# Branch hints for the expert jumps of a mixture-of-experts stage, on three engines

## What is computed

```
logits = xt @ w_router + b_router            # 256 tokens, 32 experts
top_val, top_idx = top_k(logits, 4)          # each token goes to 4 experts
gates = softmax(top_val)
for each expert e, for its tokens xb:
    hdn  = xb @ w_up[e] + b_up[e]            # 1024 -> 2048
    gate = minimum(hdn[:, :1024], 7); up = clip(hdn[:, 1024:], -7, 7)
    act  = (up + 1) * gate * sigmoid(1.702 * gate)
    y    = act @ w_down[e] + b_down[e]       # 1024 -> 1024
    out[token] += gate_of_token * y
```

## Time and profile before

| | us |
|---|---|
| median of 3 runs | 2451.59 |
| lowest and highest | 2449.55, 2455.35 |
| the profiled execution | 2454.41 |
| its span, first to last instruction | 2452.5 |
| TensorE busy | 2310.3 (94% of the span) |
| VectorE, ScalarE busy | 806.9, 487.8 |
| stage of the experts | about 1431 to 2403 |

### The profile page before, as it was taken

How to read it: one execution, slowest core, us unless ns; L and a number is a source line. 1 busy time by engine, 2 the same in 40 slices (tenths; PEclk the granted TensorE clock), 3 DMA queues, 4 the chain that set the end, 5 groups by cost and what they waited for, 6 DMA issues and landing times.

```text
span 2452.5 us, 34141 instructions
## 1 busy us (share of the span) xinstructions
PE 2310.3 (94%) x14422; PEld 1687.5 (69%) x14422; DVE 806.9 (33%) x2047; ACT 487.8 (20%) x1144; POOL 136.8 (6%) x138
## 2 busy tenths in 40 slices
PE   6888999999999789999999989999999999999997
PEld 3675788888887468887778854566566555555556
DVE  2044354577714520001665321222222222222223
ACT  2244330000013432100534120111111111111112
POOL 0000211134400000000000000000000000000000
PEclk9999999999999999999999999999999999999999
DMA  8910222124323433445233575899999999999991
GB/s 337 354 69 35 94 78 103 69 103 145 131 96 149 167 137 137 142 167 199 105 137 137 216 301 212 364 427 427 426 425 427 426 427 426 426 427 427 427 426 78
DMA packets 42115, 601.61 MB, mean 245 GB/s; under 512 B 4672, under 2 KB 5184, under 8 KB 5600
## 3 DMA queue, kind: packets, MB, share of 16 engines
q1 hardware_dynamic: 41472, 593.30, 59.8%
q10 hardware_dynamic: 480, 5.97, 0.6%
HBM read 598.20 MB, written 1.05 MB: 244 GB/s over the span
## 4 chain that ended last, share of the span: by engine, by line
PE 81%; DMA 13%; DVE 2%; ACT 2%; issue 1%; POOL 0%; SPq 0%; POOLq 0%; PEldq 0%; ACTq 0%; DVEq 0%
PE PS L1095 14%; PE PS L854 7%; PE PS L1119 7%; DMA RG<-in_w_up 7%; PE PS L633 7%; PE PS L668 6%; PE PS L617 6%; PE PS L720 5%; DMA BIG<-in_w_up 4%; PE PS L508 4%; PE PS L607 3%; PE PS L706 2%; PE PS L1028 2%; PE PS L1131 2%; PE PS L564 2%; DMA RG<-in_w_ada 1%
## 5 line engine op out<-in xcount | busy, mean ns | idle before, releaser
L2318 DVE TENSOR_SCALAR STAT<-PS 128x128 f32<-128x128 f32 (+1 forms) x128 | 37.8, 296 | 683.1 <-PE PS L1095 683.1
L1095 PE MATMUL PS<-BIG,XS 128*64 128x256 f32 (+1 forms) x2016 | 239.8, 388 | 8.3 <-DMA BIG<-in_w_up 8.0
L1095 PEld LDWEIGHTS PS<-BIG,XS 128*64 128x64 f32 (+1 forms) x2016 | 146.4, 139 | 99.8 <-issue 20.4
L1095 PE MATMUL PS<-RG,XS 128*64 128x256 f32 (+1 forms) x1520 | 180.2, 387 | 10.1 <-DMA RG<-in_w_up 10.1
L1271 ACT ACTIVATE BIG<-PS 128x256 f32<-128x256 f32 (+2 forms) x205 | 86.5, 430 | 515.1 <-PE PS L633 138.9
L854 PE MATMUL PS<-XS,RG 128*128 128x256 f32 x768 | 172.1, 382 | 5.0 <-DVE XS L1822 4.1
L1095 PEld LDWEIGHTS PS<-RG,XS 128*64 128x64 f32 (+1 forms) x1520 | 108.9, 139 | 80.4 <-DMA RG<-in_w_up 15.9
L854 PEld LDWEIGHTS PS<-XS,RG 128*128 128x128 f32 x768 | 145.6, 191 | 26.7 <-issue 6.9
L1678 ACT ACTIVATE STAT<-STAT 128x128 f32<-128x128 f32 (+1 forms) x128 | 40.1, 313 | 585.5 <-DVE STAT L2318 585.5
L617 PE MATMUL PS<-HN,RG 128*128 128x256 f32 x640 | 140.3, 382 | 4.0 <-ACT HN L1316 4.0
L1795 DVE TENSOR_SCALAR HOLD<-PS 128x256 f32<-128x256 f32 x27 | 11.4, 423 | 401.6 <-PE PS L484 299.8
(11 more groups left out here) (347 smaller groups left out, 3310.3 us busy)
## 6 DMA issues: line engine op xcount, KB each, us to landing
BIG<-in_w_up SPq DMA_DIRECT2D x64, 2048.0 KB, 30.3
RG<-in_w_up SPq DMA_DIRECT2D x48, 2048.0 KB, 30.4
RG<-in_w_ff SPq DMA_DIRECT2D x32, 2048.0 KB, 8.1
BIG<-in_w_down SPq DMA_DIRECT2D x32, 2048.0 KB, 31.2
RG<-in_w_ada SPq DMA_DIRECT2D x24, 2048.0 KB, 8.9
RG<-in_w_down SPq DMA_DIRECT2D x24, 2048.0 KB, 34.2
RG<-in_w_in SPq DMA_DIRECT2D x23, 2048.0 KB, 8.0
SM<-in_w_up SPq DMA_DIRECT2D x16, 2048.0 KB, 30.6
```

The source lines that it names most:

```text
L1095: i = pe.matmul(half_of(b, h, sides), Xg[:, k, 0:cap], w[:, k, h * wd:h * wd + wd], start=False, stop=k == 7)
```

## The change

So that 0 means "over 64 tokens", the flags are stored the other way round (`is_le` for `is_gt`), and the compare names the broad code as the target when the register is 0. The registers are renamed from `wide` to `few`. The diff for TensorE; ScalarE and VectorE have the same in their functions:

```
-            wide = [pe.alloc_register(f"pe_wide{i}") for i in range(2)]
+            few = [pe.alloc_register(f"pe_few{i}") for i in range(2)]
+            hints = {}
...
                 if ex + 1 < NEXP:
-                    pe.load(wide[(ex + 1) % 2], FLAG[0:1, ex + 1:ex + 2])
+                    pe.load(few[(ex + 1) % 2], FLAG[0:1, ex + 1:ex + 2])
+                if broad:
+                    hints[ex, "out"] = pe.mark_branch_hint_location()
+                elif ex + 1 < NEXP:
+                    hints[ex + 1] = pe.mark_branch_hint_location(few[(ex + 1) % 2])
                 if ex == BIASES:
                     biases()
...
-            pe.load(wide[0], FLAG[0:1, 0:1])
+            pe.load(few[0], FLAG[0:1, 0:1])
...
-                    pe.br_cmp(wide[ex % 2], 0, on_true=f"pe_narrow{ex}", on_false=f"pe_broad{ex}", comp_op="IS_EQ")
+                    jump = pe.br_cmp(few[ex % 2], 0, on_true=f"pe_broad{ex}", on_false=f"pe_narrow{ex}", comp_op="IS_EQ")
+                    if ex:
+                        jump.branch_hint(hints[ex])
...
                 with nc.body(f"pe_broad{ex}", parent=at, valid_engines=[mybir.EngineType.PE]):
                     expert(ex, True)
-                    pe.br(f"pe_next{ex}")
+                    pe.br(f"pe_next{ex}").branch_hint(hints[ex, "out"])
...
-            dve.tensor_scalar(FLAG[0:1, 0:32], banks[b][0:1, 64:96], 64.0, None, ALU.is_gt).then_inc(s_free[b], 1)
+            dve.tensor_scalar(FLAG[0:1, 0:32], banks[b][0:1, 64:96], 64.0, None, ALU.is_le).then_inc(s_free[b], 1)
```

More of the change, by code:

```diff
@@ L1660, in _ @@
             evac(GTT, ("gt",), rows=slice(0, 32))
-            wide = [act.alloc_register(f"act_wide{i}") for i in range(2)]
+            few = [act.alloc_register(f"act_few{i}") for i in range(2)]
+            hints = {}
             over = act.alloc_register("act_over")
@@ L1673, in expert @@
                 if ex + 1 < NEXP:
-                    act.load(wide[(ex + 1) % 2], FLAG[0:1, ex + 1:ex + 2])
+                    act.load(few[(ex + 1) % 2], FLAG[0:1, ex + 1:ex + 2])
+                if broad:
+                    hints[ex, "out"] = act.mark_branch_hint_location()
+                elif ex + 1 < NEXP:
+                    hints[ex + 1] = act.mark_branch_hint_location(few[(ex + 1) % 2])
                 for c in range(4):
@@ L1700, in _ @@
             act.load(over, FLAG[0:1, 32:33])
-            act.load(wide[0], FLAG[0:1, 0:1])
+            act.load(few[0], FLAG[0:1, 0:1])
             fork = nc.cur_bb
@@ L1707, in _ @@
                     ahead.append(nc.cur_bb)
-                    act.br_cmp(wide[ex % 2], 0, on_true=f"act_narrow{ex}", on_false=f"act_broad{ex}", comp_op="IS_EQ")
+                    jump = act.br_cmp(few[ex % 2], 0, on_true=f"act_broad{ex}", on_false=f"act_narrow{ex}", comp_op="IS_EQ")
+                    if ex:
+                        jump.branch_hint(hints[ex])
                     with nc.body(f"act_narrow{ex}", valid_engines=[mybir.EngineType.Activation]):
@@ L1739, in _ @@
                     expert(ex, True)
-                    act.br(f"act_next{ex}")
+                    act.br(f"act_next{ex}").branch_hint(hints[ex, "out"])
             with nc.body("act_dense", parent=fork, valid_engines=[mybir.EngineType.Activation]):
@@ L2271, in _ @@
             dve.tensor_tensor(GTE, GTE, c4b[:, :, 3:4].broadcast_to([128, 2, 32]), ALU.mult).then_inc(s_gts, 1)
-            wide = [dve.alloc_register(f"dve_wide{i}") for i in range(2)]
+            few = [dve.alloc_register(f"dve_few{i}") for i in range(2)]
+            hints = {}
             over = dve.alloc_register("dve_over")
@@ L2289, in expert @@
                 if ex + 1 < NEXP:
-                    dve.load(wide[(ex + 1) % 2], FLAG[0:1, ex + 1:ex + 2])
+                    dve.load(few[(ex + 1) % 2], FLAG[0:1, ex + 1:ex + 2])
+                if broad:
+                    hints[ex, "out"] = dve.mark_branch_hint_location()
+                elif ex + 1 < NEXP:
+                    hints[ex + 1] = dve.mark_branch_hint_location(few[(ex + 1) % 2])
                 if ex:
@@ L2367, in _ @@
             dve.load(over, FLAG[0:1, 32:33])
-            dve.load(wide[0], FLAG[0:1, 0:1])
+            dve.load(few[0], FLAG[0:1, 0:1])
             D = Steps(s_dvef)
@@ L2375, in _ @@
                     ahead.append((D.n, nc.cur_bb))
-                    dve.br_cmp(wide[ex % 2], 0, on_true=f"dve_narrow{ex}", on_false=f"dve_broad{ex}", comp_op="IS_EQ")
+                    jump = dve.br_cmp(few[ex % 2], 0, on_true=f"dve_broad{ex}", on_false=f"dve_narrow{ex}", comp_op="IS_EQ")
+                    if ex:
+                        jump.branch_hint(hints[ex])
                     with nc.body(f"dve_narrow{ex}", valid_engines=[mybir.EngineType.DVE]):
@@ L2422, in _ @@
                     expert(ex, True)
-                    dve.br(f"dve_next{ex}")
+                    dve.br(f"dve_next{ex}").branch_hint(hints[ex, "out"])
             D = Steps(s_dveg)
```

## The result

The kernel with the change takes 2436.72 us (median of 4 runs, 2433.08 to 2437.21); the kernel before, in runs beside it, takes 2452.8 us (4 runs, 2449.55 to 2455.35). The ratio is 0.9938, with an interval of 0.9926 to 0.9950. The medians differ by 16.1 us; the ratio and its interval stand for 15.2 us (12.3 to 18.1). The forecast was 2436.4.

What follows compares the result with a forecast made beforehand. The transfers were taken to bound the kernel from 1546 us on, with TensorE setting their start. 9.14 + 7.13 - 0.9 - 0.2 = 15.2 us off took the median from 2451.6 to 2436.4 us, range 2433 to 2445.5.

Steps and rivals of the forecast that it cites:

- The bound: From 1546 us on, unbroken weight transfers set the end, 29.5 us per narrow expert against TensorE's 27.88.
- The time to spare: From expert 2 on, TensorE could do 29 us more work in all without moving the end.
- Jump in: TensorE's compare into broad expert 1: the 5.95 us hole and slower matmuls behind it go, 9.14 us.
- late packet: Code arriving a little late at the first jump, into the broad expert: 0.2 us lost (bounds 0 and 0.5).
- Jump out: TensorE's unconditional jump from the broad expert: the 5.09 us hole and slower matmuls behind it go, 7.13 us.
- The clock: TensorE's slow clock in the broad expert may partly come back: 0.9 us taken off the gain.
- second dip: Slow clock at 1476.8 to 1480.2, behind TensorE's wait for VectorE's two copies; cost 1.73 us, half expected to stay.
- Sum: TensorE reaches expert 2, and the transfers' unbroken run starts, 15.2 us earlier; the end moves by the same.
- VectorE, ScalarE, the flags, the hints' own time: Hints on VectorE and ScalarE, reversed flags and compares, and the hint instructions themselves: 0 us at the end.
- A: No effect: the hint doesn't steer the code fetch, both holes stay, 2451.6 us; chance 12%.
- B: Half the gain: one jump helped, a late fetch, or a second fetch after arrival; 2440 to 2444.5 us; chance 20%.
- C: Slower: a "not taken" hint drops the running fetch, 5.4 us per narrow expert, +118 us, about 2570; chance 8%.

Runs made afterwards that it cites:

- The repeated gather: The changed kernel with the eight gather matmuls made twice on TensorE for experts 3 to 31; 2461.53 us, ratio 1.0056 to the kernel before.

## Why the prediction was right

**The bound.** Right. The transfers set the end, and the end moves by what their unbroken run starts earlier. The repeated gather shows the other side, 50 us of TensorE's work for 25 to 29 us of time. The time to spare was put at 29 us and measured 21 to 25.

**Jump in.** Predicted 5.95 + 1.46 + 0.37 + 1.36 = 9.14 us, less 0.9 for the clock and 0.2 for a late packet, 8.0. In the profile the hole gives 5.95, the gather 3.33 - 1.89 = 1.44, the bias 1.43 - 1.13 = 0.30, and the up projection 15.29 - 15.64 = -0.35: 7.3 us. The code came a little after the jump was reached, as reckoned from the packets (625 ns where 0.7 us was said), and the queued matmuls covered it. The assumption that the hint takes the place of the fetch in order fits as well: the packet kept its place, 27.5 us behind expert 0's compare.

**Jump out.** Predicted 5.09 + 0.54 + 1.50 = 7.13 us, and each of the three came out so. The way there was another than the one forecast. The packet just ahead of the jump was to become the narrow code; in the changed kernel there is none. Between the hint out at 1460.7 and the jump at 1515.4 code moves at 1463.8 and 1488.3, and then not before 1520.1. So the code was there at least 27 us ahead; which of the two packets held it, the rows don't say.

**The clock.** This is the term that was mis-sized. Half of the second dip's 1.73 us was to stay; all of it stayed, and 0.05 more. It cost 0.9 us of the forecast. The prediction put the dip down to the wait for VectorE's two copies, which the change leaves alone. That it stays without the long hole shows that the hole isn't its cause, but the copies alone aren't either: at expert 12 of the kernel that has two broad experts and no hint out, TensorE waits for the same two copies (0.70 us each), the granted clock is 1.00 from 1806 to 1826, and the up projection takes 13.93 us. What else it takes is open.

**Sum.** The chain gives 7.3 + 7.1 = 14.5 us from the first bias of expert 0 to the up projection of expert 2, and the whole stage 13.8. The two executions differ by 2454.41 - 2436.85 = 17.6 us. The rest of it, some 3.5 us, lies ahead of the change: the first bias of expert 0 began at 1434.94 before and at 1431.43 after, well within the spread given above. So the change is worth some 14 us where 15.2 were forecast, and the medians' 16.1 us holds some of that spread. That the forecast met the median to 0.3 us is in part luck.

**VectorE, ScalarE, the flags, the hints' own time.** Taken as 0 and measured as 0: ratios of 0.9995 and 1.0001 without TensorE's hints, and 28 to 53 ns for a hint.

**The rivals.** A is out: both holes are gone. In the kernel before, both far jumps wait for a packet that moves inside them (6837 and 7171 ns, packets at about 1467.5 and 1531), and the measured 625 and 333 ns decide against A for a hinted jump. B is out: no hole stands behind the arrival, though each of its halves exists as a kernel (2445.21 and 2442.4 us, in or near the 2440 to 2444.5 that it gave). C is out. A "not taken" hint costs nothing (2436.72 us with 29 of them, 2436.68 without), and even a wrong hint made no wait: the ten that moved code cost a packet of 0.02 MB each, and not the 5.4 us that C was priced at.

What the prediction did not have is the half-microsecond hole in each narrow expert. It was free only because the transfers were the bound by 1.6 us per expert.

## What to carry to other kernels

Look in the chain for holes put down to "issue" beside a compare or jump of several microseconds. A hint on the engine that sets the end, given an expert (29 us) ahead and not 35 instructions, removed 5 to 6 us for each far jump, and 1.4 us (jump in) and 2.0 us (jump out) of slower matmuls behind it. It was worth nothing on engines that had other cover (2451.2 us, where the kernel before takes 2452.7). Try each hint by itself, and with data that takes the rare path late as well. Here the hint for the unconditional jump back put 0.3 to 0.5 us in front of later experts and undid the hints for later jumps in, which showed only when a second expert was broad; it paid for itself only because the transfers hid that.

## What the hardware showed that was not expected

- A far jump without a hint takes 6.4 to 7.2 us on TensorE's sequencer in these runs, with the transfers at a DMA share of 0.8 to 1.0. The long compare at the very end of the program, where the share is 0.02, takes 3.3 to 3.8 us.
- A hint didn't bring its fetch forward here: at the jump in, the packet moved 27 us behind the hint (1457.8 and 1430.7), where the packet in order had been.
- A wrong hint made no wait and turned no jump: 131 packets of code for 121, compares of 68 ns for 63, and at most 1.9 us in all. Only ten of the 29 wrong hints that ran moved a further packet.
- With the hint on the jump out, things change from 142 us behind that jump on (1515.4 and 1657.5): holes of 0.3 to 0.5 us per expert, and a hinted jump of 5960 ns that takes 367 ns when that one hint is missing.
- Whether a different place in the code, or a different form of the jump back, keeps both jumps short without these holes wasn't tried.
